# Attention units of two blocks of both heads, score and value matmuls alternating between the halves of the array

## What is computed

```
def sink_softmax(s, mask, sink):
    s = jnp.where(mask, s, -jnp.inf)
    m = jnp.maximum(jnp.max(s, axis=-1, keepdims=True), sink)
    p = jnp.exp(s - m)
    return p / (jnp.sum(p, axis=-1, keepdims=True) + jnp.exp(sink - m))

def swa_prompt(q, k, v, sinks):
    ...
    kb, vb = band(k), band(v)          # each block with the block before it
    s = jnp.einsum('bnqkgd,bnjkd->bnkgqj', qb, kb,
                   preferred_element_type=jnp.float32) * (HEAD_DIM ** -0.5)
    ...
    mask = ((diff >= 0) & (diff < WINDOW) & (kpos >= 0))[None, :, None, None]
    p = sink_softmax(s, mask, sinks.astype(jnp.float32).reshape(N_KV_HEADS, GROUP, 1, 1))
    o = jnp.einsum('bnkgqj,bnjkd->bnqkgd', p.astype(v.dtype), vb)
```

## Time and profile before

| what | value |
|---|---|
| median of three runs | 3382.32 us (3379.57 to 3382.58) |
| span of the profiled execution | 3378.6 us, so the median lies 3.7 us above it |
| PE busy | 3197.5 us (95%) |
| POOL, DVE, ACT busy | 1551.1, 1511.2, 854.5 us |
| attention stage | about 1860 to 2930 us of the span, 16 pairs |

### The profile page before, as it was taken

How to read it: one execution, slowest core, us unless ns; L and a number is a source line. 1 busy time by engine, 2 the same in 40 slices (tenths; PEclk the granted TensorE clock), 3 DMA queues, 4 the chain that set the end, 5 groups by cost and what they waited for, 6 DMA issues and landing times.

```text
span 3378.6 us, 50475 instructions
## 1 busy us (share of the span) xinstructions
PE 3197.5 (95%) x19117; PEld 3077.4 (91%) x19117; DVE 1511.2 (45%) x1745; ACT 854.5 (25%) x1708; POOL 1551.1 (46%) x1153
## 2 busy tenths in 40 slices
PE   7999999999899999999778999999999999999995
PEld 6999999999899999999668998999899899899995
DVE  6999999999711131000560433244323343500043
ACT  5121121121222132212321322222222222332232
POOL 2777877878543324333353223332233223144475
PEclk9999999999899999999899999999999999899998
DMA  4122122122132252212453112111111211333386
GB/s 158 45 64 58 46 69 58 46 69 58 57 100 87 93 171 78 73 63 70 170 190 94 36 37 63 41 37 44 47 47 41 53 38 46 118 114 87 97 295 217
DMA packets 171677, 284.87 MB, mean 84 GB/s; under 512 B 62008, under 2 KB 72504, under 8 KB 171576
## 3 DMA queue, kind: packets, MB, share of 16 engines
q1 hardware_dynamic: 127328, 222.48, 22.2%
q10 hardware_dynamic: 41912, 52.32, 4.2%
q0 software_dynamic: 2352, 8.88, 0.7%
HBM read 218.44 MB, written 67.15 MB: 85 GB/s over the span
## 4 chain that ended last, share of the span: by engine, by line
PE 57%; POOL 17%; issue 12%; DVE 6%; DMA 4%; ACT 2%; SPq 1%; POOLq 0%; ACTq 0%; DVEq 0%
PE z_odd L512 9%; PE z_odd L513 8%; PE z_odd L515 8%; PE z_even L512 8%; PE z_even L513 7%; PE z_even L515 7%; POOL w_lo L1013 6%; POOL work L1094 4%; PE aux L609 3%; POOL work L1086 3%; PE z_even L627 2%; DMA work<-conv_scratch 1%; PE z_even L629 1%; POOL work L1122 1%; DMA work<-out_scratch 1%
## 5 line engine op out<-in xcount | busy, mean ns | idle before, releaser
L1013 POOL TENSOR_TENSOR w_lo<-w_raw,w_hi 128x512 fp32r<-128x512 f32 x528 | 746.7, 1423 | 1452.1 <-ACT w_hi L730 1451.6
L512 PE MATMUL z_even<-u_hi,w_hi 128*128 128x364 f32 (+1 forms) x2784 | 925.1, 332 | 80.7 <-POOL u_lo L1174 33.8
L512 PE MATMUL z_odd<-u_hi,w_hi 128*128 128x364 f32 (+1 forms) x2784 | 939.0, 337 | 58.9 <-POOL w_lo L1013 58.9
L513 PE MATMUL z_odd<-u_lo,w_hi 128*128 128x364 f32 (+1 forms) x2784 | 922.5, 331 | 0.0
L513 PE MATMUL z_even<-u_lo,w_hi 128*128 128x364 f32 (+1 forms) x2784 | 921.0, 331 | 0.0
L730 ACT ACTIVATE w_hi<-w_raw 128x512 fp32r<-128x512 f32 x528 | 331.4, 630 | 1730.5 <-PE z_even L515 810.3
L515 PE MATMUL z_odd<-u_hi,w_lo 128*128 128x364 f32 (+1 forms) x2784 | 636.5, 330 | 0.0
L515 PE MATMUL z_even<-u_hi,w_lo 128*128 128x364 f32 (+1 forms) x2784 | 635.3, 329 | 0.0
L512 PEld LDWEIGHTS z_even<-u_hi,w_hi 128*128 128x128 f32 x2784 | 529.8, 190 | 99.6 <-issue 30.7
L512 PEld LDWEIGHTS z_odd<-u_hi,w_hi 128*128 128x128 f32 x2784 | 531.7, 191 | 97.3 <-POOL w_lo L1013 55.1
L513 PEld LDWEIGHTS z_odd<-u_lo,w_hi 128*128 128x128 f32 x2784 | 532.1, 191 | 0.1
(11 more groups left out here) (148 smaller groups left out, 2405.1 us busy)
## 6 DMA issues: line engine op xcount, KB each, us to landing
w_raw<-in_w SPq DMA_DIRECT2D x528, 256.0 KB, 2.7
work<-in_x SPq DMA_DIRECT2D x32, 544.0 KB, 5.7
work<-branch_scratch SPq DMA_DIRECT2D x31, 544.0 KB, 5.5
conv_scratch<-work ACTq DMA_DIRECT2D x16, 544.0 KB, 2.7
work<-conv_scratch SPq DMA_DIRECT2D x16, 544.0 KB, 3.7
resid_scratch<-work ACTq DMA_DIRECT2D x16, 544.0 KB, 6.2
branch_scratch<-work ACTq DMA_DIRECT2D x16, 512.0 KB, 2.6
branch_scratch<-work POOLq DMA_DIRECT2D x15, 544.0 KB, 3.0
```

The lines of the kernel that those rows point to most:

```text
L512: pe.matmul(o, w_hi[:, q, at:at + P], chunk(u_hi[:, k, :], c), start=(i == 0), stop=False)
L513: pe.matmul(o, w_hi[:, q, at:at + P], chunk(u_lo[:, k, :], c), start=False, stop=False)
L1013: pool.tensor_tensor(w_lo[:, q, :], w_raw[:, q, :], w_hi[:, q, :].bitcast(F32), ALU.subtract).then_inc(w_lo_ready, 1)
```

## The change

A unit is now two blocks (2u and 2u + 1) of both heads. Quarter 2 p + bl of `s_qk`, `sc`, `pc` and `pp` holds head p and block 2u + bl, so that each head has its own PSUM bank of `s_qk`. Consecutive score matmuls take turns between rows 0 to 63 and 64 to 127, consecutive value matmuls between array columns 0 to 63 and 64 to 127. Only unit 0 now contains block 0 (twice), and the softmax steps read two sinks per unit. Sample scores and values go over the samples in order, taking turns between the heads, and all values with cached keys come before all with new keys. `LINKS_J` counts one DVE step less.

```diff
+        def per_head(ap):
+            return ap.rearrange("p (h b) k -> p h b k", h=2)
...
             def scores(g, jj, u):
-                p, hh = u % 2, u // 2
                 pe.wait_ge(s_free, 17 * g + 4 * jj + u + 1)
-                for i in range(4):
-                    b = 4 * hh + i
+                for bl in range(2):
+                    b = 2 * u + bl
                     lo = BLK if b == 0 else 0
-                    mm = pe.matmul(s_qk[:, i, lo:2 * BLK], qf[HD * p:HD * p + HD, BLK * b:BLK * b + BLK],
-                                   kd[HD * p:HD * p + HD, BLK * (b - 1) + lo:BLK * b + BLK], start=True, stop=True)
+                    for p in range(2):
+                        mm = pe.matmul(s_qk[:, 2 * p + bl, lo:2 * BLK],
+                                       qf[HD * p:HD * p + HD, BLK * b:BLK * b + BLK],
+                                       kd[HD * p:HD * p + HD, BLK * (b - 1) + lo:BLK * b + BLK],
+                                       start=True, stop=True)
                 mm.then_inc(s_done, 1)
...
             def values(g, jj, u):
-                p, hh = u % 2, u // 2
+                def o(p, b):
+                    return z_even[HD * p:HD * p + HD, 1 + b // 4, BLK * (b % 4):BLK * (b % 4) + BLK]
                 pe.wait_ge(pt_read, 17 * g + 4 * jj + u + 2)
-                for i in range(4):
-                    b = 4 * hh + i
-                    o = z_even[HD * p:HD * p + HD, 1 + hh, BLK * i:BLK * i + BLK]
-                    mm = pe.matmul(o, vd[:, b, :], pc[:, i, :], start=True, stop=(b == 0))
+                for bl in range(2):
+                    b = 2 * u + bl
+                    for p in range(2):
+                        mm = pe.matmul(o(p, b), vd[:, b, :], pc[:, 2 * p + bl, :], start=True, stop=(b == 0))
                     if b > 0:
-                        mm = pe.matmul(o, vd[:, b - 1, :], pp[:, i, :], start=False, stop=True)
+                        for p in range(2):
+                            mm = pe.matmul(o(p, b), vd[:, b - 1, :], pp[:, 2 * p + bl, :], start=False, stop=True)
                 mm.then_inc(pv_done, 1)
...
             def sample_scores(g):
-                for i in range(4):
-                    p, bh = i // 2, i % 2
-                    rows = slice(HD * p, HD * p + HD)
-                    for r in range(4):
-                        b = 4 * bh + r
-                        pe.matmul(s_qk[32 * r:32 * r + 32, i, 0:P], qs_m[rows, b, :], kc[rows, b, :], ...)
-                        mm = pe.matmul(s_qk[32 * r:32 * r + 32, i, P:P + SS], qs_m[rows, b, :], ...)
+                for b in range(SB):
+                    bh, r = b // 4, b % 4
+                    for p in range(2):
+                        rows = slice(HD * p, HD * p + HD)
+                        pe.matmul(s_qk[32 * r:32 * r + 32, 2 * p + bh, 0:P], qs_m[rows, b, :], kc[rows, b, :], ...)
+                    for p in range(2):
+                        rows = slice(HD * p, HD * p + HD)
+                        mm = pe.matmul(s_qk[32 * r:32 * r + 32, 2 * p + bh, P:P + SS], qs_m[rows, b, :], ...)
...
             def sample_values(g):
-                for i in range(4):
-                    p, bh = i // 2, i % 2
-                    for r in range(4):
-                        b = 4 * bh + r
-                        o = z_even[HD * p:HD * p + HD, 1, 32 * b:32 * b + 32]
-                        pe.matmul(o, vc[:, b, :], pp[:, i, 32 * r:32 * r + 32], start=True, stop=False)
-                        mm = pe.matmul(o, vn[0:SS, b, :], pc[0:SS, i, 32 * r:32 * r + 32], start=False, stop=True)
+                for b in range(SB):
+                    for p in range(2):
+                        pe.matmul(o(p, b), vc[:, b, :], pp[:, 2 * p + b // 4, 32 * (b % 4):32 * (b % 4) + 32],
+                                  start=(b == 0), stop=False, skip_group_check=True)
+                for b in range(SB):
+                    for p in range(2):
+                        mm = pe.matmul(o(p, b), vn[0:SS, b, :],
+                                       pc[0:SS, 2 * p + b // 4, 32 * (b % 4):32 * (b % 4) + 32],
+                                       start=False, stop=(b == SB - 1), skip_group_check=True)
...
             def copy_prev(g, jj, u):
-                first = 1 if u // 2 == 0 else 0
-                act.activation(sc[u][:, first:4, :], s_qk[:, first:4, 0:BLK], ACT.Copy).then_inc(s_copied, 1)
+                if u == 0:
+                    act.activation(per_head(sc[u])[:, :, 1, :], per_head(s_qk)[:, :, 1, 0:BLK], ACT.Copy
+                                   ).then_inc(s_copied, 1)
+                else:
+                    act.activation(sc[u], s_qk[:, :, 0:BLK], ACT.Copy).then_inc(s_copied, 1)
...
             def row_max(g, jj, u):
-                sink = cols[:, bass.ds(C_SINK + 8 * g + 2 * jj + u % 2, 1)]
-                if u // 2 == 0:
-                    link(dve.memset(sc[u][:, 0, :], NEG))
+                sink = cols[:, bass.ds(C_SINK + 8 * g + 2 * jj, 2)].unsqueeze(2).to_broadcast([P, 2, 2])
+                two = lambda a: st[:, a:a + 4].rearrange("p (a b) -> p a b", a=2)
+                if u == 0:
+                    link(dve.memset(per_head(sc[u])[:, :, 0, :], NEG))
...
-                link(dve.tensor_scalar(st[:, 0:4], st[:, 0:4], HD ** -0.5, sink, ALU.mult, ALU.max))
+                link(dve.scalar_tensor_tensor(out=two(0), in0=two(0), scalar=HD ** -0.5, in1=sink,
+                                              op0=ALU.mult, op1=ALU.max))
                 link(dve.tensor_scalar(st[:, 4:8], st[:, 0:4], -1.0, None, ALU.mult))
-                dve.tensor_scalar(st[:, 8:12], st[:, 4:8], sink, None, ALU.add).then_inc(max_ready, 1)
+                dve.tensor_tensor(two(8), two(4), sink, ALU.add).then_inc(max_ready, 1)
...
-            LINKS_J = 4 * (3 + 2 + 1) + 2
+            LINKS_J = 4 * (3 + 2 + 1) + 1
```

More of the change, by code:

```diff
@@ L637, in sample_scores @@
                 pe.sem_inc(pe_passed, 1)
-                for i in range(4):
-                    p, bh = i // 2, i % 2
-                    rows = slice(HD * p, HD * p + HD)
-                    for r in range(4):
-                        b = 4 * bh + r
-                        pe.matmul(s_qk[32 * r:32 * r + 32, i, 0:P], qs_m[rows, b, :], kc[rows, b, :],
+                for b in range(SB):
+                    bh, r = b // 4, b % 4
+                    for p in range(2):
+                        rows = slice(HD * p, HD * p + HD)
+                        pe.matmul(s_qk[32 * r:32 * r + 32, 2 * p + bh, 0:P], qs_m[rows, b, :], kc[rows, b, :],
                                   start=True, stop=True)
-                        mm = pe.matmul(s_qk[32 * r:32 * r + 32, i, P:P + SS], qs_m[rows, b, :],
+                    for p in range(2):
+                        rows = slice(HD * p, HD * p + HD)
+                        mm = pe.matmul(s_qk[32 * r:32 * r + 32, 2 * p + bh, P:P + SS], qs_m[rows, b, :],
                                        kd[rows, TP + SS * b:TP + SS * b + SS], start=True, stop=True)
@@ L652, in sample_values, with o @@
                 pe.sem_inc(pe_passed, 1)
-                for i in range(4):
-                    p, bh = i // 2, i % 2
-                    for r in range(4):
-                        b = 4 * bh + r
-                        o = z_even[HD * p:HD * p + HD, 1, 32 * b:32 * b + 32]
-                        pe.matmul(o, vc[:, b, :], pp[:, i, 32 * r:32 * r + 32], start=True, stop=False)
-                        mm = pe.matmul(o, vn[0:SS, b, :], pc[0:SS, i, 32 * r:32 * r + 32], start=False, stop=True)
+                def o(p, b):
+                    return z_even[HD * p:HD * p + HD, 1, 32 * b:32 * b + 32]
+                for b in range(SB):
[7 more added lines that the diff above has]
+                                       start=False, stop=(b == SB - 1), skip_group_check=True)
                 mm.then_inc(pv_done, 1)
```

## The result

The kernel takes 3278.74 us (median of 4 runs, 3273.48 to 3282.49) where the one before, beside it on the same chip, took 3381.69 (4 runs): a ratio of 0.9694 [0.968, 0.9708]. The forecast was 3278 us. The profiled execution took 3278.45 us with a span of 3276.8, so 101.8 us less than the span of before.

A forecast was written before the change was run, and what follows sets the result against it. PE, busy 95% of the span, was taken as the bound. Twelve pairs without samples give 55 us, four with samples 49: 104 us off 3378.6 gives 3274.6, plus 3.7 for the median 3278 us; range 3250 to 3308.

The forecast's parts named there:

- Overlap: Scores and values on PE: both array halves stream at once, saving 3.3 us each, 6.6 of 67 a pair.
- rows don't overlap: Scores on PE: row halves run one after another, only columns overlap; 3.1 us a pair, 3305 us; chance 0.07.
- every change of half costs a pause: Scores and values on PE: 0.1 us lost per change, nothing overlaps; 3.8 us a pair slower, 3443 us; chance 0.04.
- Program order: PE's queue: passes leave strictly in order, so halves overlap only partly; 4.1 us a pair, 3290 us; chance 0.08.
- Waits: PE ahead of turns 1 and 2: idle 0.8 and 1.1 us because ACT and DVE keep their pace.
- small edits: DVE's softmax chain: merged memset under 0.3 us; two lines change form, losing nothing or gaining 0.14 a unit, taken as nothing.
- PSUM Bottleneck: Emptying of PSUM: not sped up by tiling, may become the bound; without the waits twelve pairs give 79 us, not 55.
- the rival: DVE's L1410, 0.90 us in unit 1: if also in units 0 and 2, a pair keeps 3.2 us; 3300 us; chance 0.13.
- If it never does: DVE's L1410 never slow: waits shrink to 0.1 and 0.4 us, 6.1 us a pair, 3257 us; chance 0.10.
- gross sum of 6.6: PE's scores and values in a pair: 3.3 us saved in each, before waits for ACT and DVE.
- The 2.64 us of idle time behind it stay (issue).: PE behind the sample values: the idle time keeps its length of 2.64 us.
- The term for the clock: Pairs with samples: a shorter thin stretch shortens the 10.4 us at 1.2 GHz, worth 0 to 1.5 us, taken as 0.5.

The follow-up runs named there:

- two runs in series: Changed kernel with a semaphore holding the second half until the first is done, in scores alone (3337.44 us) or in values alone (3337.86 us).
- grouped run: Changed kernel with all matmuls of one half issued before those of the other, in scores and in values: 3305.18 us.
- gains-first run: Changed kernel with POOL's four gain multiplications of a tile ahead of its four subtractions, instead of by turns: 3259.22 us.
- two-input form: Changed kernel with DVE's negation L1429 as -2x + x in one scalar_tensor_tensor instead of a tensor_scalar by -1: 3278.88 us.

## Why the prediction was right, and where not

**Overlap: right.** Full overlap of both kinds gave 1.04 and 1.01 us for scores 3 and values 2; they took 1.06 and 1.03. The two runs in series lost what the passes, the semaphore and the waits make it. The rivals "rows don't overlap" and "every change of half costs a pause" fall with these rows.

**Program order: refuted in its strict form.** The Trainium skill ("TensorE: Matmul & The Clock Gate", The mechanism) has matmuls leave in strict order. In the grouped run a pass starts 0.013 us after one that stands four places ahead in the same queue, so the trace disagrees. But the grouped values, 0.49 us late, show a limit to that, which the prediction did not have: about four passes of one half in a row. The alternation is needed for values, with eight passes to a half, and not for scores, with four.

**Waits: right in place and releaser, too long.** Forecast were 0.8 and 1.1 us ahead of turns 1 and 2, measured 0.32 and 0.75, both released by `read_turned`. Counted from the start of copy 0, copies 2 and 3 should have come after 10.17 and 14.87 us; by ACT's rows they came after 9.83 and 14.30. The mis-sized step is the small edits: "each unit's chain may lose nothing or gain 0.14; I take nothing". L1427 took 0.16 us (0.25 in units 1 and 3) and L1430 0.16, where L1411 took 0.23 and L1409 in the second pair 0.23 to 0.24. That is 0.14, 0.05 and 0.14 us in the units ahead of copy 3, 0.33 of its 0.57. Another 0.18 come from ACT: the prediction let copies 1 and 3 start at the end of the last record of the exps before them, but a copy whose scores are there starts 0.09 us sooner (1923.53 against 1923.43 + 0.19). The last 0.06 stay open. A pair gained 5.04 us, not 4.6. It takes 60.3 us and not "about 62.4" because the 67.00 us window of the earlier trace rows is longer than a pair, 65.32.

The Trainium skill's rule that the prediction cited ("TensorEngine Tiling (Array Packing)", PSUM Bottleneck) fits these waits only in part. PE does wait for `read_turned`, which empties PSUM. But with the gains first its two instructions take 0.68 and 0.69 us as they did, and the waits are gone: what made it late was the negation, which does not touch PSUM. The pair is 1.45 us shorter there, 1.06 of it the waits.

**The slow negation: half of the rival.** The prediction saw L1410 at 0.90 us in unit 1 and asked what happened if units 0 and 2 had it too. They did not; units 1 and 3 kept it, and the forecast held. "If it never does", it said, 6.1 us a pair; the gains-first run made that case and measured 65.32 - 58.83 = 6.5, the gross sum of 6.6 nearly whole.

**Samples: the step that was mis-sized.** "The 2.64 us of idle time behind it stay (issue)." It became 5.11. The prediction took the pause as a length of its own behind the last matmul. It is the rest of a jump back that starts when the branch is issued, while the passes still run: shorter passes uncover more of it. The sample values themselves came as costed (2.17 us, forecast 2.6), but of the 6.2 us from their start to the next matmul only 11.48 - 7.27 = 4.2 were gained in the first group. The term for the clock, 0.5 us gained, did not come. The stretch at 1.2 GHz is shorter, 6.83 us instead of 10.24, but more of it now lies on the projections behind the sample values, 4.7 us instead of 3.2. The windows view from the first of these to the next pair's scores 0, before and after, gives the length, PE's busy time and the clock:

```profile
2105.28:2133.70 28.42, 28.41 (x162) 0.94 0.27 63
2080.30:2109.39 29.09, 29.09 (x162) 0.92 0.26 73
```

That is 0.7 us lost in the first group (0.3 and 0.7 in the next two). A smaller term went the other way: up to the sample values the pair gained 6.2 us, not 5.8. In the first group 6.2 + 4.2 - 0.7 make the 9.8 measured within rounding, where the prediction had 12.5. The four pairs gave 41.9 us, not 49.

**The sum.** 60.5 + 41.9 = 102.4 against 55 + 49 = 104: two errors of 5.5 and 7 us that cancel. That the time came out within 1 us of the forecast is luck, since its terms were off by several.

## What to carry to other kernels

Work that uses half the rows or half the columns of the array can be put beside the other half's for nothing, if the passes of the two halves alternate closely enough in the program: here four of one half in a row did no harm, six and eight did. Before counting a shortened stretch as gained, ask what runs beside it that was hidden: here it was a loop's jump back, counted from its issue, and unrolling the loop gave 11 us. And when a chain is late by some tenths of a microsecond, look at what another engine does in just that microsecond: reordering POOL's list, with no work less, gave 19.5 us.

## What the runs showed of the hardware

- PE starts passes for another part of the array ahead of those queued before them. With four passes of one half in a row the halves start 0.013 us apart (grouped scores), with six 0.28 and with eight 0.49 (grouped values); the sample scores start four strips by 2077.50, with the first pass of the fourth twelve places behind that of the first.
- The jump back of PE's outer loop took 3.3 to 5.2 us here, that of its inner loop 0.21 to 0.22, and a branch that does not jump 0.07 to 0.08.
- A DVE instruction on four elements took 0.97 us instead of 0.17 beside POOL's gain, in three forms, and ended with it. The Trainium skill ("GPSIMD Engine Reference", Key points) says that POOL and DVE share interfaces to SBUF and collide when DVE runs in a mode with two ports or has two SBUF inputs. The two-input form agrees with it at 0.96 us; for one tensor with a constant, held at 0.97, no row here shows in which mode it ran. POOL's subtraction L1030 holds DVE in the same way: L1427 ended 0.02 us behind it in 32 units. It cost only 0.1 us because the subtraction was nearly done. Not every DVE instruction is held: the reduction L1426 took 0.69 us beside L1030 and alone.
- 64 passes of 32 columns took 8.84 us where 128 and 8 rows came by turns and one half of the array behind the other, and 2.17 where the rows change once and the halves alternate. The two parts were not taken apart.
